# Memory values moved from the attention loop into the stick-breaking attention, memory keys behind every second attention unit

## The reference

```
y_b = nsa_mixer(...)                 # per head and query tile: compressed, selected and windowed keys
y_c = mla_mixer(...)                 # causal attention of 96-wide heads
y_d = stick_breaking_mixer(...)      # z = q k; log_1m = log_sigmoid(-z); rem = suffix sums of log_1m
                                     # a = exp(log_sigmoid(z) + rem); y = a v
y = rms_norm(concat(y_a, y_b, y_c, y_d)); x = x + y @ w_out
...
# second block, much later:
mem_n = rms_norm(mem);  k, v = split(mem_n @ w_kv)     # 256 x 1024 each
```

## Time and profile before

| | us |
|---|---|
| median of 3 runs | 2051.49 (2047.72 to 2051.57) |
| the profiled execution, its own time | 2053.02 |
| its span, first to last instruction | 2050.9 |
| PE busy in that span | 1872.5 (91%) |
| the 64 units of attention | 271.3 to 458.1 |
| stick-breaking attention on PE | 458.8 to 516.9 |
| norms of the outputs, until the first product with `w_out` | 516.9 to 529.1 |

### The profile page before, as it was taken

The page is one execution under the profiler, slowest core; times in us unless marked ns, Lnnn a source line. Parts: engine busy times, 40 slices in busy tenths (PEclk is TensorE's granted clock), DMA queues, the critical chain, the costliest instruction groups (busy, mean ns, idle before and its releaser), DMA issues.

```text
span 2050.9 us, 20976 instructions
## 1 busy us (share of the span) xinstructions
PE 1872.5 (91%) x8142; PEld 1410.5 (69%) x8142; DVE 830.9 (41%) x1418; ACT 734.5 (36%) x1328; POOL 693.8 (34%) x376
## 2 busy tenths in 40 slices
PE   5998799998989989997989989997989989999996
PEld 3775546674668878885856667775667768887784
DVE  3312134444324004443245577784323154444343
ACT  4142032236434442323334444444233332223322
POOL 3342000000344443444322255552332434444343
PEclk7999559998999999998989999999999999999998
DMA  4422201111123322232211111111411113323221
GB/s 156 107 87 82 80 2 62 62 59 45 42 90 103 98 87 86 99 103 72 82 42 62 52 33 40 52 52 42 144 62 63 62 62 103 100 85 103 82 82 41
DMA packets 122195, 152.23 MB, mean 74 GB/s; under 512 B 8779, under 2 KB 110561, under 8 KB 121458
## 3 DMA queue, kind: packets, MB, share of 16 engines
q1 hardware_dynamic: 118016, 136.80, 21.1%
q0 software_dynamic: 2384, 11.76, 1.6%
q10 hardware_dynamic: 1698, 2.35, 0.3%
HBM read 144.90 MB, written 6.00 MB: 74 GB/s over the span
## 4 chain that ended last, share of the span: by engine, by line
PE 73%; issue 11%; POOL 6%; DVE 5%; ACT 4%; ACTq 1%; DMA 0%; POOLq 0%; DVEq 0%
PE bank L1733 37%; PE bank L1783 14%; POOL w_low L616 4%; PE bank L1106 3%; POOL acc L779 2%; PE bank L1938 2%; PE bank L1490 2%; PE bank L1057 2%; PE bank L1941 2%; PE bank L968 2%; PE bank L2034 1%; PE bank L1890 1%; PE bank L976 1%; DVE act_low L814 1%; PE bank L699 1%
## 5 line engine op out<-in xcount | busy, mean ns | idle before, releaser
L616 POOL TENSOR_TENSOR w_low<-ring,w_high 128x1024 fp32r<-128x1024 f32 x224 | 542.0, 2420 | 947.6 <-ACT w_high L599 947.6
L1733 PE MATMUL bank<-act_high,w_high 128*128 128x512 f32 (+1 forms) x1344 | 547.5, 407 | 26.4 <-DVE act_low L814 23.5
L1733 PE MATMUL bank<-act_high,w_low 128*128 128x512 f32 (+1 forms) x1344 | 531.1, 395 | 0.0
L1733 PE MATMUL bank<-act_low,w_high 128*128 128x512 f32 (+1 forms) x1344 | 530.8, 395 | 0.0
L599 ACT ACTIVATE w_high<-ring 128x1024 fp32r<-128x1024 f32 x224 | 235.5, 1053 | 364.1 <-PE bank L1783 203.4
L1733 PEld LDWEIGHTS bank<-act_high,w_high 128*128 128x128 f32 (+1 forms) x1344 | 256.4, 191 | 104.9 <-issue 37.6
L1733 PEld LDWEIGHTS bank<-act_high,w_low 128*128 128x128 f32 (+1 forms) x1344 | 256.2, 191 | 55.4
L1733 PEld LDWEIGHTS bank<-act_low,w_high 128*128 128x128 f32 (+1 forms) x1344 | 257.3, 191 | 49.9 <-issue 1.9
L866 DVE TENSOR_TENSOR act_low<-arena,act_high 128x512 fp32r<-128x512 f32 x73 | 133.2, 1841 | 235.0 <-ACT act_high L860 235.0
L1783 PE MATMUL bank<-act_high,w_high 128*128 128x512 f32 x432 | 172.4, 399 | 17.3 <-DVE act_low L866 9.8
L1783 PE MATMUL bank<-act_low,w_high 128*128 128x512 f32 x432 | 171.4, 397 | 0.0
(11 more groups left out here) (317 smaller groups left out, 2328.0 us busy)
## 6 DMA issues: line engine op xcount, KB each, us to landing
ring<-in_ffn_w SPq DMA_DIRECT2D x32, 1024.0 KB, 5.3
ring<-in_w_in SPq DMA_DIRECT2D x28, 1024.0 KB, 5.3
ring<-in_w_up SPq DMA_DIRECT2D x22, 1024.0 KB, 5.1
ring<-in_w_down SPq DMA_DIRECT2D x11, 1024.0 KB, 5.0
ring<-in_w_mem_kv SPq DMA_DIRECT2D x8, 1024.0 KB, 5.3
ring<-in_cmp_w SPq DMA_DIRECT2D x4, 1024.0 KB, 5.7
ring<-in_w_out SPq DMA_DIRECT2D x4, 1024.0 KB, 5.4
ring<-in_w_mix_out SPq DMA_DIRECT2D x4, 1024.0 KB, 5.1
```

Source lines behind the costliest of these rows:

```text
L616: nc.gpsimd.tensor_tensor(part(w_low, name), raw_part(name), part(w_high, name).bitcast(F32), ALU.subtract).then_inc(w_split, 1)
L1733: last = nc.tensor.matmul(b[0:rows, :], w[:, k, 0:rows], a, start=k == 0 and n == 0, stop=k == KT - 1 and n == 2)
```

## The change

Three things are changed, none of which changes what is computed.

1. The pieces of the memory keys stand behind every second unit: behind unit u, if u is even, piece u / 2. ACT copies key tile m at unit 8 (m + 1), the last one behind the loop.
2. The pieces of the memory values stand in the stick-breaking attention: one behind each score of heads 1 to 3, and one behind each of the four steps of the sums of every head, the last four behind the sums of head 3, ahead of its values. DVE copies `memv{h}` behind the shifts of head h. The value tiles use banks 4 and 6.
3. ACT rounds the first two parts of `w_out` behind the stick-breaking attention, not ahead of it.

```
         for m in range(8):
             plan(f"memk{m}", "act", f"mkv{m // 2}", m % 2 == 1)
+        use_banks(4, 6)
...
-        def stick_scores(eng, h):
+        def stick_scores(eng, h, between=None):
             for kt in range(TT):
...
+                if between:
+                    between(eng, kt)
...
-        def stick_sums(eng, h):
+        def stick_sums(eng, h, between):
...
                 last.then_inc(sb_c, 1)
+                between(eng, kt)
...
-            attend_pe(eng, 0, N_B1, ahead_by=2, between=mem_pair)
+            def mem_key_pair(eng, u):
+
+                if u % 2 == 0:
+                    mem_pair(eng, u // 2)
+
+            attend_pe(eng, 0, N_B1, ahead_by=2, between=mem_key_pair)
             eng.wait_ge(head_out, 4)
             stick_scores(eng, 0)
             for h in range(4):
                 if h + 1 < 4:
-                    stick_scores(eng, h + 1)
-                stick_sums(eng, h)
+                    stick_scores(eng, h + 1, lambda eng, kt: mem_pair(eng, 32 + 8 * h + kt))
+                stick_sums(eng, h, lambda eng, kt: mem_pair(eng, 36 + 8 * h + kt - (4 if h == 3 else 0)))
+                if h == 3:
+                    for piece in range(60, 64):
+                        mem_pair(eng, piece)
                 stick_values(eng, h)
...
-                if u % 4 == 1 and 5 <= u <= 33:
-                    m = (u - 5) // 4
+                if u % 8 == 0 and u:
+                    m = u // 8 - 1
                     take(f"memk{m}", mem_k1[:, 256 * m:256 * (m + 1)], w=256)
 
             attend_act(eng, 0, N_B1, pair_end_b1, take_mem_k)
-            round_weights(eng, "wo1")
+            take_mem_k(eng, N_B1)
             stick_logs(eng, 0)
...
                 if h % 2:
                     take_stick(eng, h // 2)
+            round_weights(eng, "wo1")
...
-            attend_dve_early(eng, 0, N_B1, take_mem_v)
-            take_mem_v(eng, N_B1)
+            attend_dve_early(eng, 0, N_B1)
             stick_softplus(eng, 0)
             for h in range(4):
                 if h + 1 < 4:
                     stick_softplus(eng, h + 1)
                 stick_shift(eng, h)
+                take(f"memv{h}", mem_v1.rearrange("p (t d) -> p t d", d=D)[:, :, 256 * h:256 * h + 256])
```

More of the change, by code:

```diff
@@ L1147, in attend_act, with attend_dve_early @@
                 pair_end(eng, u)
-        def attend_dve_early(eng, u0, u1, between):
+        def attend_dve_early(eng, u0, u1, between=None):
             shift(eng, u0)
@@ L1160, in attend_dve_early @@
                     copy_turned(eng, u)
-                between(eng, u)
+                if between:
+                    between(eng, u)
         def attend_dve(eng, u0, u1, between=None):
```

## The result

| | before | changed | ratio, 95% interval |
|---|---|---|---|
| first set, 8 and 8 runs | 2051.59 (2047.72 to 2057.71) | 2043.12 (2035.14 to 2044.75) | 0.9946 [0.9926, 0.9966] |
| the changed kernel again, 16 and 7 runs | 2052.99 (2047.54 to 2060.13) | 2043.93 (2041.30 to 2046.53) | 0.9949 [0.9932, 0.9967] |

The forecast was -2.7 us; measured are -8.5 and -9.1. The time lies inside the range of 2041 to 2056, and the sign was right, but the forecast's own case, a change within 0.2%, is not what happened: the gain is three times the forecast one.

A forecast was written before the change was run, and what follows sets the result against it. PE was taken to bound the attention, while the stick-breaking attention had some 10 us of holes on PE. Attention -32.2, stick-breaking attention +26.5 and +3.0 behind it gave -2.7 us, median 2051.5 to 2048.8, range 2041 to 2056.

The forecast's parts named there:

- the forecast's own case: Whole kernel: -2.7 us, median 2048.8, own range 2045 to 2053, chance 0.50; about what a measurement can't tell from no change.
- Pieces out of the attention and the clock there: Attention: 32 odd units lose their pieces, -36.7 us; clock rising at unit 8 instead of 6 costs +4.5; together -32.2.
- Rival 1: Attention: unit 6 raises the clock as before, so the +4.5 us is gone: -7.2, 2044.3 us; chance 0.20.
- the 3.4 us of unit 6: Attention, unit 6: transposes, values and a piece without 64-row scores, taken as the stretch the clock's rise at 305.0 followed.
- the price of 1.06 us: Cost of one piece on PE at 2.4 GHz, from 309.92 to 310.98 in the attention; 29 units priced at it, 30.7 us.
- PE still bounds the attention: Attention: DVE and ACT chains, about 21 us a sparse head against PE's 26.2, cost nothing, covered by even units' pieces.
- Rival 4: Attention: DVE and ACT become the bound, each odd unit waiting 0.3 us, +9.6: +6.9, 2058.4 us; chance 0.08.
- Scores of head 0: Stick-breaking attention, head 0: ACT is free earlier, one key tile copy replacing two roundings ahead of `stick_logs`; -0.6 us.
- Scores of head 1: Stick-breaking attention: four pieces at 2.0 us, at 1.2 GHz, fill the hole; 6.4 us becomes 13.1, +6.7.
- rival 2: Stick-breaking attention: being busy is enough, so head 1's scores run mostly at full clock: -8.0, 2043.5 us; chance 0.10.
- Sums of head 0, heads 1, 2 and 3: Stick-breaking attention with added pieces: sums of head 0 +3.2 us, heads 1 and 2 +9.0 together, head 3 +8.2.
- Behind it: Behind the stick-breaking attention: ACT's two roundings ahead of the squares +2.0 us, earlier clock fall +1.0; values' store hidden.

The follow-up runs named there:

- second execution: Second profiled execution of the changed kernel, run again unaltered (`e0_after_again`), clock rising at the end of unit 8; 2046.53 us.
- e1_keys_front: Changed kernel with the 32 key pieces one behind each of units 0 to 31, none behind units 32 to 63; 2056.1 us, 1.0023 of before.
- e4_grouped: Changed kernel with the four value pieces of each scores section (heads 1 to 3) together behind the third score; two executions, 2033.2 and 2040.8 us.
- e3_round_early: Changed kernel with ACT's two roundings of weights moved ahead of the last head's exponentials; median 2042.0 us.
- e10_scale_early: Changed kernel with one edit: DVE scales the memory input ahead of the norms of the mixers; median 2041.4 us.
- first execution: First profiled execution of the changed kernel, clock rising at the end of unit 6; 2035.14 us.

## Why the prediction was off, point by point

- *Pieces out of the attention and the clock there*, -32.2: measured -30.9 in the second execution, with the rise at the end of unit 8 as forecast. Rival 1, the rise at unit 6, happened in one of six profiled executions (I gave 0.20): -35.1. The number is close, but two readings under it were not sound. First, I called the 3.4 us of unit 6 the only stretch since 276 without narrow scores. The trace of before has a longer one just ahead of it, 296.38 to 300.05, 3.67 us, and the clock didn't rise there:

```profile
296.38 0.69 PE L1057 MATMUL bank<-const_sb,prob 128*128 128x128 f32 x2
297.00 1.12 PE L1106 MATMUL bank<-prob_t,arena 128*64 128x128 f32 x4
```

  So such a stretch alone doesn't raise it, and that unit 8 came out is in part luck. Second, the price of 1.06 us doesn't hold in the latent attention. From its first score on nine pieces fewer saved 47.31 - 39.57 = 7.7 us, 0.86 each, not 1.06, 1.8 in all: 411.52 to 458.83 in before, 389.64 to 429.21 in the second execution:

```profile
411.52 0.39 PE L973 MATMUL bank<-arena 96*128 96x128 f32 x2
```

```profile
389.64 0.49 PE L974 MATMUL bank<-arena 96*128 96x128 f32 x2
429.21 1.12 PE L1198 MATMUL bank<-arena 64*128 64x512 f32 x2 [0.69 <-ACT arena L1120]
```

  In the sparse units behind unit 8 the price was right: 19 pieces fewer saved 20.0 us, 1.05 each.
- *PE still bounds the attention*: right, PE is busy for 119.26 of the 120.0 us behind the rise in the second execution. The bare units of `e1_keys_front` show what the chain costs when it isn't covered: 1.4 us in 32 units. Rival 4, at 9.6, was too dear.
- *Scores of head 0*, -0.6: measured -0.56. *Scores of head 1*, +6.7: measured +6.9, at a clock of 0.50 throughout. The number was right, and with it rival 2 fell: PE was busy for 13.32 of 13.32 us there. The Trainium skill, TensorE: Matmul & The Clock Gate, section What's actually happening, says that the clock follows how busy PE has been. By the profile's busy time the trace disagrees, here and above all in the 23.90 us of `e1_keys_front`; that busy time counts an instruction from start to end, and no run here shows how much of it the array worked. The same section says that the point of the rise varies between runs of one kernel; the executions with unit 6 and unit 8 agree with that.
- *Sums of head 0, heads 1, 2 and 3*, +3.2, +4.5, +4.5 and +8.2, in all 20.4: measured +1.1, +3.2, +3.2 and +6.3, in all 13.8. This is the step that failed: it is 6.6 us too dear, where the whole forecast missed the second execution by 6.0 (-2.7 against -8.7); the attention (+1.3), the scores of heads 0 and 1 (+0.3) and the norms (-1.0) make up the difference. The term that was mis-sized is the price of a piece, 1.06 us, taken from a piece beside 64-row scores in the attention and used for the 20 pieces among the 128-row sums as well. What a step of the sums costs without a piece is in the timeline of before, head 3, its last step and the end of the one ahead:

```profile
513.52 0.39 PE L1210 MATMUL bank<-arena,const_sb 128*128 128x128 f32 x2
514.15 0.49 PE L1207 MATMUL bank<-arena,const_sb 128*128 128x128 f32 x2 [0.25 <-DVE arena L1251]
514.57 2.37 PE L1217 MATMUL bank<-arena 128*64 128x512 f32 x8
```

  And with pieces, the changed kernel's second execution, head 1 at full clock:

```profile
471.88 0.39 PE L1214 MATMUL bank<-arena,const_sb 128*128 128x128 f32 x2
472.10 1.03 PE L1946 MATMUL bank<-ring,mem_high 128*128 128x256 f32 x4
472.96 0.38 PE L1211 MATMUL bank<-arena,const_sb 128*128 128x128 f32 x2
473.18 1.03 PE L1946 MATMUL bank<-ring,mem_high 128*128 128x256 f32 x4
474.14 2.37 PE L1222 MATMUL bank<-arena 128*64 128x512 f32 x8
```

  A piece takes 0.86 us here (472.10 to 472.96), and the sum ahead of the last piece 0.22, where before it took 0.42 ahead of the values. All four steps took 4.87 us before (509.45 to 514.57 less 0.25 of idle) and 7.88 with four pieces: 0.75 us a piece. Four such pieces in each of three heads, 3 x 4 x (1.06 - 0.75) = 3.7, and eight in head 3, which cost 6.3 instead of 8.2, make 5.6 of the 6.6 us. The rest is mostly the clock: I gave the sums of head 0 two slow microseconds, and it came back 0.4 us into them. `e4_grouped` agrees from the other side: pieces put together cost 0.91 where pieces among 64-row scores cost 1.06. That the rows of the neighbours are what sets the price is my reading of these rows; why they should isn't shown.
- *Behind it*, +3.0: measured +2.0. The roundings were on the path in full (`e3_round_early` gives back 2.0); the 1.0 for an earlier fall of the clock wasn't paid: the stretch had 0.88 in both executions. It can be, though: `e10_scale_early`, with the same code there, had 0.78 and took 15.2 us, the forecast's number. The store of the values hid, as said: in the first execution it was issued at 497.01 and landed 6.9 us later, and DVE wrote over that memory only at 510.44.
- *The sum*. With the pieces among the sums at what they cost and nothing else altered the forecast would have been -2.7 - 5.6 = -8.3, against the measured -8.5 and -9.1. Part of this agreement is luck: the attention was 1.3 us too favourable and the norms 1.0 too dear, and they nearly cancel.

## What to carry to other kernels

Price a moved instruction by the neighbours it will have, not by those it has: here the same four matmuls cost 1.06, 0.91, 0.86 or 0.75 us. And ask of each piece of filler what it holds up besides its own cover: in these kernels the clock stayed at 2.4 GHz through narrow units with a 128-row piece behind every second one and fell without it, and a few such pieces in a row, where it was down, had it back 27 us earlier in the attention (6.4 against 33.7 behind the first score) and 7 us earlier in the scores of head 1. A stretch that the profile shows busy throughout can still lose the clock.

## What the hardware showed that I had not expected

- PE lost the clock while busy, by the profile, for 82.00 of 82.00 us, and stayed at 1.2 GHz for a stretch busy for 23.90 of 23.90 (`e1_keys_front`).
- Executions of the same code raise the clock at different points: 27.3 us behind the first score in one, 36.7 to 37.1 in five.
- The cost of four fp32 matmuls of 256 columns over 128 rows at 2.4 GHz: 1.06 us between 64-row scores, 0.91 in a row of their kind, 0.86 net in the latent attention with its 96-row scores, 0.75 net between 128-row sums.
- Executions of one kernel differ by up to 16 us (2049.2 to 2065.1 in `e1_keys_front`, 2047.5 to 2060.1 in before), and the first score of the attention lies anywhere from 266.7 to 272.5 us though the code ahead of it is the same in these kernels. Where that comes from is open.
